# Expert gate and up weights read in 8 KB runs, and one activation table for exponential and logarithm, in a hybrid attention/GLA/MoE step

## Chip, cores and metric

The kernel runs on one core of a Trainium2 chip. A time is what the device takes for one execution, in microseconds (us); timed runs are given as their median. A profile is one further execution, recorded by the hardware profiler; its times are us from the start of its span. TensorE is PE in the profile (its weight loads PEld), VectorE is DVE, ScalarE is ACT, GpSimd is POOL, SyncE is SP; a name with a q at its end (SPq, POOLq) is that engine's instruction queue.

## The reference, cut to what matters

One layer of an encoder for 256 prompt tokens and 8 x 16 sample tokens, 384 in all, with D = 2048. All arrays are float32.

```
sh1, sc1, gt1, sh2, sc2, gt2 = split(silu(c) @ w_ada + b_ada)        # adaLN, w_ada 2048 x 12288
h = rmsnorm(x) * (1 + sc1) + sh1
z = h @ w_in                                                        # 2048 x 4368
group A: sliding-window attention with sinks
group B: lg = log_sigmoid(ab @ w_gate_up + b_gate) / 16             # decay of the gated linear attention
         b = cumsum(lg);  q*exp(b), k*exp(-b), recurrence over blocks of 16
x = x + gt1 * (concat(A, rmsnorm_head(B) * silu(r)) @ w_out)
h = rmsnorm(x) * (1 + sc2) + sh2
router: softmax over 4 groups, best group; in it the best 2 of 8 experts, softmax over the two
expert e: (silu(h @ w_eg[e]) * (h @ w_eu[e])) @ w_ed[e]             # 2048 x 512, 2048 x 512, 512 x 2048
x = x + gt2 * (sum over the two experts of gate * expert)
y = rmsnorm(x) * g_final
```

Every norm is an inverse root of a mean square. There are 32 experts; the kernel reads the weights of all of them, 12.6 MB each.

## The kernel before

Each engine has its program, written out by hand, and waits on semaphores. The order of the work is therefore the order in each engine's program.

**The ring.** All weights pass through `ring`, in units of 1 MiB (128 partitions x 8 KB, `unit(s)`). Before the experts it has 8 units (`PRE`), in the expert stage 12 (`RING`, `UE`), one expert's worth: units 0 to 3 are the gate weights, 4 to 7 the up weights, 8 to 11 the down weights. SyncE issues one DMA a unit (`fetch`, line 332, for adaLN, input and output projection; `expert`, line 392, for the experts) and waits before each on `unit_used`, which TensorE raises when it has used the unit's last bytes. A unit of expert e is thus requested when the same unit of expert e - 1 has been used. The first expert's 12 units are requested before the router has finished.

**Gate and up weights.** The view `eg_v` takes row k*128 + p of a 2048 x 512 matrix to partition p; `quad(j)` receives four neighbouring k, so each partition gets four runs of 512 floats (2 KB). The adaLN and down weights come as one run of 2048 floats (8 KB) per partition.

**The expert loop.** GpSimd gathers an expert's rows by an indirect DMA into `xg[u]` (up to 64 slots; a row's two halves of 1024 columns on partitions 0 to 63 and 64 to 127). TensorE transposes it in eight steps (`rows_T`, line 1081), ScalarE and VectorE copy the result into `xeT[u]` (lines 1339 and 1797), whose index is chunk c, half q, slot s. `up` (line 1097) multiplies: for unit j and its part kk_, `k = 4 * (j % 4) + kk_`, the rows are chunk `k % 8` of half `k // 8`. ScalarE takes the exponential (line 1343), VectorE makes silu times up (lines 1802 to 1805), TensorE transposes the hidden rows (line 1105), and `down` (line 1117) multiplies them by the down weights. Results are copied (lines 1810 and 1354) and scattered by GpSimd. TensorE's order is: up of e, transposes of e + 1, hidden transpose of e, down of e. The loops over a data-dependent overflow count follow; in the profiled run they aren't entered.

**ScalarE and its tables.** ScalarE computes exponentials and logarithms by a table that has to be loaded first. No load is written in the program: they are put in when it is built. An inverse root is `inv_rms` (lines 1154 and 1157): exp(-0.5 * ln(mean)), refined by five small steps on VectorE (`refine`, lines 1414 to 1418). It is used at the first norm, three times for the heads (`head_norms`), ahead of the experts, and three times at the end, once for each block of 128 tokens. Log-sigmoid (`log1p_exp`, lines 1253 to 1255) is |x|, exp, ln, once for each block; `decay_exps` (lines 1269, 1270) follows.

**The end.** VectorE combines the experts' outputs of each block (lines 1857 to 1859) and then refines the norm of the block before; for blocks 0 and 1 ScalarE multiplies by the norm (line 1399) and GpSimd by the gain (line 650), for block 2 VectorE does both (line 1852). GpSimd issues the output DMAs (line 652).

Of the kernel before, what the change touches and what calls it, by code (L numbers as in the profile page):

```python
# [103 lines left out]
def encoder_step(nc, A, O):  # L104
    with ExitStack() as ctx:
# [50 lines left out]
        def unit(s):  # L156
            return ring[:, s * D:(s + 1) * D]
# [124 lines left out]
        out_v = w_out.rearrange("(k p) c -> p k c", p=P)  # L282
        eg_v = A["w_expert_gate"][0].rearrange("e (k p) f -> p e k f", p=P)
        eu_v = A["w_expert_up"][0].rearrange("e (k p) f -> p e k f", p=P)
        ed_v = A["w_expert_down"][0].rearrange("e (k p) d -> p e k d", p=P)
# [34 lines left out]
        def _(sp):  # L320
# [49 lines left out]
            def expert(e, first):  # L370

                for j in range(UE):
# [12 lines left out]
                    if j < 8:  # L385
                        src = (eg_v if j < 4 else eu_v)[:, bass.ds(e, 1), 4 * (j % 4):4 * (j % 4) + 4, :]
                        src = src.rearrange("p e k f -> p (e k) f")
                        dst = quad(j)
                    else:
                        src = ed_v[:, bass.ds(e, 1), j - 8, :].rearrange("p e d -> p (e d)")  # L390
                        dst = unit(j)
# [8 lines left out]
            with sp.If(n_over > 0):  # L400
                with sp.Fori(0, n_over) as i:
                    e = sp.value_load(ov_i[0:1, bass.ds(i + 1, 1)], min_val=0, max_val=NE - 1)
                    for j in range(UE):
                        sp.wait_ge(unit_used, U_MOE + UE * (NE - 1) + UE * i + j + 1)
                        if j < 8:
                            src = (eg_v if j < 4 else eu_v)[:, bass.ds(e, 1), 4 * (j % 4):4 * (j % 4) + 4, :]
                            src = src.rearrange("p e k f -> p (e k) f")
                            dst = quad(j)
                        else:
                            src = ed_v[:, bass.ds(e, 1), j - 8, :].rearrange("p e d -> p (e d)")  # L410
                            dst = unit(j)
                        sp.dma_start(dst, src).then_inc(loaded[j], 16)
# [246 lines left out]
        def _(pe):  # L659
# [418 lines left out]
            def rows_T(u, e, gat_need):  # L1078
                pe.wait_ge(gat[u], gat_need)
                for c in range(8):  # L1080
                    last = tr(bank[c // 4][:, (c % 4) * P:(c % 4 + 1) * P], xg[u][:, c * P:(c + 1) * P], ident[:, :])  # L1081
                last.then_inc(eT_ps, 1)
# [63 lines left out]
        def _(act):  # L1146
# [4 lines left out]
            def inv_rms(sq, n_done, cols, out, n):  # L1151
# [5 lines left out]
                af(rs[:, 0, out], rs[:, 0, out], ACT.Exp, scale=-0.5).then_inc(rstd, 1)  # L1157

            rcount = [0]
            act.wait_ge(cT_ps, 1)  # L1160
# [732 lines left out]
```

## Time and profile before

| | |
|---|---|
| median of 3 timed runs | 2103.36 us (2103.22 to 2106.18) |
| the profiled execution | 2098.72 us, of which the span is 2097.1 us |
| mean granted TensorE clock | 0.913 of full speed |
| TensorE busy | 1637.1 us (78%) |
| VectorE, ScalarE, GpSimd busy | 379.5, 233.1, 175.6 us |
| moved by DMA | 602.96 MB in 213,869 packets, 288 GB/s over the span |
| TensorE matmuls of line 1097 (gate and up) | 485.1 us |
| TensorE matmuls of line 1117 (down) | 270.0 us |
| gate, up, down weights: request to landing | 19.0, 15.4, 15.3 us (128 units each) |

The span falls into a stage in which the adaLN weights stream in (to about 112 us), the input projection and attention (to about 610), the gated linear attention (to about 710), the output projection (729 to 896), norm and router (to 1001), the experts (1001 to 2033) and the end. The page cuts the span in 40 equal slices of 52.4 us, and gives for each the busy share in tenths and the transfer rate. The DMA share is the mean over 16 DMA engines; it can pass 1 where transfers overlap. The chain of waits is followed back from the last instruction, and credits each stretch to whoever released the next; it does not say what would have been late next.

### The profile page before, as it was taken

How to read it: one execution, taken by the hardware profiler on the slowest of the kernel's cores; microseconds unless marked ns; L12 is line 12 of the kernel's file. 1: busy time of each engine (PE TensorE's matmuls, PEld its weight loads, DVE VectorE, ACT ScalarE, POOL GpSimd, SP SyncE). 2: the span in 40 equal slices, each digit the busy share in tenths (PEclk: the TensorE clock that was granted, in tenths of full speed). 3: DMA queues.
4: the chain of work that ended last, by engine and by line, in shares of the span. 5: the costliest groups of instructions: out<-in, count | busy, mean ns of one | idle time of the engine just before them, and what ended most of it. 6: DMA issues, size and time to landing. Idle time of an engine off the chain costs nothing.

```text
span 2097.1 us, 22209 instructions
## 1 busy us (share of the span) xinstructions
PE 1637.1 (78%) x8832; PEld 820.6 (39%) x8832; DVE 379.5 (18%) x815; ACT 233.1 (11%) x532; POOL 175.6 (8%) x350
## 2 busy tenths in 40 slices
PE   4689999999977499985887787777877777777750
PEld 0155554444445244444443343333333333343320
DVE  1010000051824300044101101011010110101105
ACT  2110000000543100021000000000000000000004
POOL 5020000000020100002011010010100101011002
PEclk9799999999988699955899999999999999999985
DMA  9975666223970521161899999999999999999973
GB/s 330 404 259 226 258 247 247 97 99 110 412 267 13 180 94 67 40 240 41 316 399 396 398 393 397 397 396 399 393 397 395 396 398 390 398 396 396 397 278 143
DMA packets 213869, 602.96 MB, mean 288 GB/s; under 512 B 18485, under 2 KB 20597, under 8 KB 182713
## 3 DMA queue, kind: packets, MB, share of 16 engines
q1 hardware_dynamic: 197362, 559.13, 70.4%
q0 software_dynamic: 15648, 36.94, 5.1%
q10 hardware_dynamic: 816, 6.29, 0.7%
q8 instruction: 29, 0.48, 0.1%
q14 instruction: 14, 0.11, 0.0%
HBM read 595.42 MB, written 28.10 MB: 297 GB/s over the span
## 4 chain that ended last, share of the span: by engine, by line
PE 48%; DMA 37%; DVE 8%; ACT 3%; issue 2%; SPq 1%; POOL 1%; POOLq 0%; DVEq 0%; ACTq 0%
DMA ring<-in_w_expert_up 22%; PE bank L1117 9%; PE bank L1016 8%; PE bank L736 8%; PE bank L748 8%; DMA ring<-in_w_expert_gate 7%; PE bank L1097 6%; DMA ring<-in_w_ada 5%; DVE hbuf L1803 2%; PE bank L686 2%; DMA ring<-in_w_in 1%; PE bank L717 1%; DMA xbuf<-in_x_sample 1%; SPq L392 1%; PE bank L1105 1%
## 5 line engine op out<-in xcount | busy, mean ns | idle before, releaser
L1097 PE MATMUL bank<-ring,zbuf 128*64 128x256 f32 x4096 | 485.1, 385 | 137.6 <-DMA ring<-in_w_expert_up 113.1
L1097 PEld LDWEIGHTS bank<-ring,zbuf 128*64 128x64 f32 x4096 | 283.6, 138 | 346.9 <-DMA ring<-in_w_expert_up 165.5
L1117 PE MATMUL bank<-ring,hbuf 128*64 128x512 f32 x1024 | 270.0, 688 | 17.0 <-ACT hbuf L1351 17.0
L736 PE MATMUL bank<-hbuf,ring 128*128 128x384 f32 x512 | 166.1, 487 | 7.3 <-DMA ring<-in_w_in 4.4
L1016 PE MATMUL bank<-ring,hbuf 128*128 128x512 f32 x384 | 166.9, 598 | 5.7 <-DVEq L1678 5.7
L748 PE MATMUL bank<-ring,hbuf 128*128 128x512 f32 x384 | 165.8, 593 | 4.8 <-ACT xbuf L1202 3.5
L1117 PEld LDWEIGHTS bank<-ring,hbuf 128*64 128x64 f32 x1024 | 82.8, 157 | 184.7 <-issue 183.3
L686 PE MATMUL bank<-ring,dbuf 128*32 128x512 f32 x768 | 110.0, 681 | 49.2 <-DMA ring<-in_w_ada 49.2
L736 PEld LDWEIGHTS bank<-hbuf,ring 128*128 128x128 f32 x512 | 96.9, 190 | 77.5 <-issue 8.0
L1802 DVE TENSOR_SCALAR hbuf<-hbuf 128x256 f32<-128x256 f32 x32 | 9.4, 294 | 607.2 <-ACT hbuf L1343 607.2
L1016 PEld LDWEIGHTS bank<-ring,hbuf 128*128 128x128 f32 x384 | 73.6, 192 | 99.8 <-issue 92.5
L748 PEld LDWEIGHTS bank<-ring,hbuf 128*128 128x128 f32 x384 | 72.6, 190 | 98.1 <-issue 92.1
L607 POOL CAST cur<-stab 128x1 int32 (+1 forms) x32 | 5.8, 180 | 927.3 <-DVE zbuf L1810 927.3
L1343 ACT ACTIVATE hbuf<-bank 128x256 f32<-128x256 f32 x32 | 12.3, 385 | 597.4 <-PE bank L1097 597.4
L1105 PE MATMUL bank<-ident,hbuf 128*128 128x128 f32 x64 | 15.7, 331 | 79.5 <-DVE hbuf L1805 79.5
L1810 DVE COPY zbuf<-bank 128x512 f32<-128x512 f32 x32 | 22.1, 691 | 288.1 <-PE bank L1117 288.1
L686 PEld LDWEIGHTS bank<-ring,dbuf 128*32 128x32 f32 x768 | 19.5, 115 | 105.9 <-DMA ring<-in_w_ada 70.9
L1803 DVE RECIPROCAL hbuf<-hbuf 128x256 f32<-128x256 f32 x32 | 56.1, 1753 | 1.1
L1081 PE MATMUL bank<-ident,zbuf 128*128 128x128 f32 x264 | 36.9, 284 | 19.3 <-DMA zbuf<-h_rows,cur 19.3
L1354 ACT COPY zbuf<-bank 128x512 f32<-128x512 f32 x32 | 18.8, 586 | 276.5 <-PE bank L1117 276.5
L1081 PEld LDWEIGHTS bank<-ident,zbuf 128*128 128x128 f32 x264 | 29.0, 143 | 33.2 <-issue 33.2
L1105 PEld LDWEIGHTS bank<-ident,hbuf 128*128 128x128 f32 x64 | 7.0, 152 | 87.1 <-DVE hbuf L1805 87.1
(368 smaller groups left out, 1109.8 us busy)
## 6 DMA issues: line engine op xcount, KB each, us to landing
ring<-in_w_expert_gate SPq DMA_DIRECT2D x128, 1024.0 KB, 19.0
ring<-in_w_expert_up SPq DMA_DIRECT2D x128, 1024.0 KB, 15.4
ring<-in_w_expert_down SPq DMA_DIRECT2D x128, 1024.0 KB, 15.3
ring<-in_w_ada SPq DMA_DIRECT2D x96, 1024.0 KB, 11.8
ring<-in_w_in SPq DMA_DIRECT2D x34, 1024.0 KB, 10.5
ring<-in_w_out SPq DMA_DIRECT2D x16, 1024.0 KB, 5.1
ring<-y_rows ACTq DMA_DIRECT2D x3, 2048.0 KB, 12.1
h_rows<-zbuf POOLq DMA_DIRECT2D x3, 1024.0 KB, 5.6
```

Source lines behind the costliest of these rows:

```text
L392: sp.dma_start(dst, src).then_inc(loaded[j], 16)
L686: last = mm(bank[b][32 * q:32 * q + 32, :], cT[:, k, :], unit(n % PRE)[:, q * QN:(q + 1) * QN], start=(k == 0), stop=(k == KC - 1))
L717: last = mm(bank[t][:, 0:256], hT[:, k, t * P:(t + 1) * P], w[:, kk_, :], start=(k == 0), stop=(k == KC - 1))
L736: last = mm(bank[c][:, 0:TOK], w[:, kk_, c * P:(c + 1) * P], hT[:, k, :], start=(k == 0), stop=(k == KC - 1))
L748: last = mm(bank[t][:, :], hT[:, k, t * P:(t + 1) * P], w[:, kk_, :], start=(k == 0), stop=(k == KC - 1))
L1016: last = mm(bank[3 * b + t][:, :], hT[:, k, t * P:(t + 1) * P], w[:, kk_, :], start=(k == 0), stop=(k == KC - 1))
L1081: last = tr(bank[c // 4][:, (c % 4) * P:(c % 4 + 1) * P], xg[u][:, c * P:(c + 1) * P], ident[:, :])
L1097: last = mm(bank[2 + u][64 * q:64 * q + 64, 256 * (j // 4):256 * (j // 4) + 256], xeT[u][:, k % 8, k // 8, :], w[:, kk_, 256 * q:256 * q + ...
L1105: last = tr(bank[4][:, c * P:(c + 1) * P], hid[u][:, c * P:(c + 1) * P], ident[:, :])
L1117: last = mm(bank[5 + n][64 * q:64 * q + 64, :], hidT[u][:, k % 2, k // 2, :], unit(8 + k)[:, 1024 * q + QN * n:1024 * q + QN * n + QN], st ...
L1803: link(v.reciprocal(sg[u], sg[u]))
L1810: cp(ysb[u][:, 0:QN], bank[5][:, :]).then_inc(y_v, 1)
```

## The change

Two edits that don't touch each other.

1. Gate and up weights: the row of a matrix is now split as (g, p, r, c) with g and r of 2, p of 128 and c of 4, so that partition p gets rows 1024 g + 8 p + 4 r + c. Unit j holds g = j % 4 // 2 and r = j % 2: the four values of c are four neighbouring rows, one run of 2048 floats (8 KB), of every 16 KB. So that the columns of x meet the same rows, `rows_T` transposes columns at a step of 8: chunk c of the transposed rows is columns c, c + 8, c + 16, ... of the half. `up` is unchanged.
2. ScalarE asks once, before its first exponential, for the table set that has both exponential and logarithm.

```diff
-        eg_v = A["w_expert_gate"][0].rearrange("e (k p) f -> p e k f", p=P)
-        eu_v = A["w_expert_up"][0].rearrange("e (k p) f -> p e k f", p=P)
+        eg_v = A["w_expert_gate"][0].rearrange("e (g p r c) f -> p e g r (c f)", g=2, r=2, c=4)
+        eu_v = A["w_expert_up"][0].rearrange("e (g p r c) f -> p e g r (c f)", g=2, r=2, c=4)
...
                     if j < 8:
-                        src = (eg_v if j < 4 else eu_v)[:, bass.ds(e, 1), 4 * (j % 4):4 * (j % 4) + 4, :]
-                        src = src.rearrange("p e k f -> p (e k) f")
-                        dst = quad(j)
+                        src = (eg_v if j < 4 else eu_v)[:, bass.ds(e, 1), j % 4 // 2, j % 2, :].rearrange("p e f -> p (e f)")
+                        dst = unit(j)
...
             def rows_T(u, e, gat_need):
                 pe.wait_ge(gat[u], gat_need)
+                rows = xg[u].rearrange("p (n c) -> p c n", c=8)
                 for c in range(8):
-                    last = tr(bank[c // 4][:, (c % 4) * P:(c % 4 + 1) * P], xg[u][:, c * P:(c + 1) * P], ident[:, :])
+                    last = tr(bank[c // 4][:, (c % 4) * P:(c % 4 + 1) * P], rows[:, c, :], ident[:, :])
                 last.then_inc(eT_ps, 1)
...
+            nc.scalar.preload_act_table_set("natural_log_exp_and_others")
             rcount = [0]
             act.wait_ge(cT_ps, 1)
```

The load of the overflow loop is changed in the same way.

## Rows read from the trace of the kernel before

**Rows 1.** The page, 40 slices: DMA busy tenths and GB/s.

```profile
DMA  9975666223970521161899999999999999999973
GB/s 330 404 259 226 258 247 247 97 99 110 412 267 13 180 94 67 40 240 41 316 399 396 398 393 397 397 396 399 393 397 395 396 398 390 398 396 396 397 278 143
```

**Rows 2.** Who waited for whom: us in total, times, longest us.

```profile
PE bank L1097 <- DMA ring<-in_w_expert_up: 113.1, 113, 2.3
```

**Rows 3.** Chain of waits: start us, us, what (longest pieces, whole span).

```profile
1028.95 13.84 PE bank L1097 x128
1055.83 13.84 PE bank L1097 x128
...
1147.45 16.57 DMA ring<-in_w_expert_up
...
1409.89 16.58 DMA ring<-in_w_expert_up
```

**Rows 4.** Windows: us, busy us (count) by engine, PEclk, DMA share, GB/s.

```profile
72.97:92.88 19.91, 13.76 (x80) 3.68 (x80) 0.69 (x1) 2.35 (x4) 0.00 (x0) 0.83 1.01 421
1147.40:1409.80 262.40, 200.33 (x1362) 99.39 (x1360) 33.43 (x48) 15.44 (x32) 22.30 (x49) 0.95 1.04 396
...
1030.00:1060.00 30.00, 27.05 (x204) 14.77 (x202) 4.18 (x6) 1.93 (x4) 5.42 (x11) 0.94 1.04 396
```

**Rows 5.** Windows of 2 us inside one expert, the same columns.

```profile
1396.00:1398.00 2.00, 0.75 (x7) 0.51 (x5) 1.78 (x2) 0.74 (x2) 0.00 (x0) 1.00 1.00 411
...
1404.00:1406.00 2.00, 2.00 (x12) 0.74 (x10) 0.00 (x0) 0.00 (x0) 0.00 (x0) 1.00 1.04 384
...
1416.00:1418.00 2.00, 1.13 (x12) 0.46 (x8) 0.00 (x0) 0.00 (x0) 0.00 (x0) 1.00 1.03 356
...
1426.00:1428.00 2.00, 1.48 (x14) 1.05 (x16) 0.00 (x0) 0.00 (x0) 0.00 (x0) 1.00 1.03 430
```

**Rows 6.** Chain of waits just before the experts.

```profile
998.22 1.96 PE bank L1081 x8
```

**Rows 7.** ScalarE, groups by line: count, busy us, mean ns, idle us before.

```profile
L1154 ACT ACT_TABLE_LOAD x8 | 10.3, 1283 | 0.1
L1157 ACT ACT_TABLE_LOAD x8 | 10.3, 1283 | 0.1
...
L1255 ACT ACT_TABLE_LOAD x3 | 3.8, 1283 | 0.1
...
L1254 ACT ACT_TABLE_LOAD x2 | 2.6, 1283 | 0.0
...
L1161 ACT ACT_TABLE_LOAD x1 | 1.3, 1283 | 1.0 <-PEq L1882 1.0
L1269 ACT ACT_TABLE_LOAD x1 | 1.3, 1283 | 0.0
```

**Rows 8.** Timeline, gated linear attention: start us, us, instruction, [idle before it <-releaser].

```profile
626.01 3.78 PE L876 MATMUL bank<-modr,ring 128*128 128x512 f32 x4 [7.97 <-ACT ring L1270]
```

**Rows 9.** Timeline, first refining step at head norms and at the expert norm.

```profile
655.50 0.16 DVE L1414 TENSOR_SCALAR rs<-stat 128x4 f32<-128x4 f32 x1
...
668.78 0.17 DVE L1414 TENSOR_SCALAR rs<-stat 128x4 f32<-128x4 f32 x1 [1.56 <-ACT rs L1157]
...
689.23 0.17 DVE L1414 TENSOR_SCALAR rs<-stat 128x4 f32<-128x4 f32 x1 [0.58 <-ACT rs L1157]
...
905.85 0.17 DVE L1414 TENSOR_SCALAR rs<-stat 128x3 f32<-128x3 f32 x1 [2.96 <-ACT rs L1157]
```

**Rows 10.** Timeline, the end of the kernel.

```profile
2064.93 4.68 POOL L650 TENSOR_TENSOR xbuf<-xbuf,hbuf 128x2048 f32<-128x2048 f32 x1 [29.74 <-ACT xbuf L1399]
2065.29 6.47 DVE L1858 TENSOR_TENSOR ring<-ring,dbuf 128x2048 f32<-128x2048 f32 x1
...
2077.10 4.50 POOL L650 TENSOR_TENSOR xbuf<-xbuf,hbuf 128x2048 f32<-128x2048 f32 x1 [6.54 <-ACT xbuf L1399]
...
2082.06 0.15 DVE L1414 TENSOR_SCALAR rs<-stat 128x1 f32<-128x1 f32 x1 [7.14 <-ACT rs L1157]
```

More of the change, by code:

```diff
@@ L405, in _ @@
                         if j < 8:
-                            src = (eg_v if j < 4 else eu_v)[:, bass.ds(e, 1), 4 * (j % 4):4 * (j % 4) + 4, :]
-                            src = src.rearrange("p e k f -> p (e k) f")
-                            dst = quad(j)
+                            src = (eg_v if j < 4 else eu_v)[:, bass.ds(e, 1), j % 4 // 2, j % 2, :].rearrange("p e f -> p (e f)")
+                            dst = unit(j)
                         else:
```

## The prediction

> **What bounds the kernel now.** I read the page's slices first, since they show at a glance which resource is full where [rows 1]. From slice 21 to slice 38 the DMA digit is 9 and the rate stays at 390 to 399 GB/s: nearly half of the span is one stage, the 32 experts, and it runs at the pace of the transfers. The waits say the same from the other side: TensorE, at the gate and up matmuls of line 1097, waits mostly for up weights that have not landed [rows 2]. So the first part of the change (how gate and up weights are read) bears on the bound of the longest stage, and the second part (table loads on ScalarE) does not bear on that stage at all, because the expert loop uses only the exponential and copies.
>
> The chain of waits gives the lengths that I need. The piece that begins with the landing of an up weight repeats every expert; from 1147.45 to 1409.89 [rows 3] lie eight experts (the window over them counts 1362 TensorE instructions [rows 4], and an expert has 128 + 32 + 8 + 2 = 170), so one takes 262.4 / 8 = 32.8 us. The same chain holds a stretch in which TensorE did not have to wait, because the ring of 12 units had been filled ahead: expert 1 starts its gate matmuls at 1028.95 and expert 2 at 1055.83, so TensorE with its hidden-layer wait needs 26.9 us an expert. The transfers need 32.8, TensorE 26.9: the cover is 5.9 us an expert.
>
> **Part 1: the pieces.** A gate or up unit is 1 MiB (1.049 MB). Before, it is four runs of 2 KB for each partition, after, one run of 8 KB. The destination, the matmuls, the number of DMAs (12 an expert) and the bytes are the same. What does a unit cost in either form? For 8 KB runs the trace has the adaLN weights: from 72.97 to 92.88 the stage takes hardly anything else, and the window over these eight units shows 421 GB/s [rows 4], that is 19.91 / 8 = 2.49 us a unit. For the mix of the expert stage, the window over the eight experts shows 396 GB/s at a DMA share of 1.04. 32.8 us at 396 GB/s are 12.99 MB, of which the 12 units are 12.58; the 0.41 MB left are the gathered and scattered rows, 1.0 us. If the four down units (8 KB runs already) cost what the adaLN units do, 4 x 2.49 = 10.0 us, then the eight gate and up units cost 32.8 - 10.0 - 1.0 = 21.8 us, or 2.73 us each, 384 GB/s. Two-microsecond windows inside one expert bear this out: 384 GB/s where gate and up units are moving, and 411 and 430 at the times when down units are [rows 5].
>
> After the change all 12 units are of the 8 KB form: 12 x 2.49 + 1.0 = 30.9 us an expert, 1.92 less before rounding. 31 experts are loaded while the stage runs (the first lies in the ring before it starts): 31 x 1.92 = **60 us**. Is the new period still that of the transfers? TensorE needs 26.9, so 4.0 us of cover are left of 5.9. That number was taken at a granted clock of 0.94 (the window that begins at 1030 [rows 4]), no better than the 0.95 of the stage, so it is not flattered by the clock. Does the queue run dry when it moves faster? At the moment the last up unit lands, TensorE has consumed everything before it, so nearly the whole ring, twelve units or 30 us of work, is outstanding; the pause for the hidden layer (about 6 us) is far shorter. So the faster transfer is worth its full amount until TensorE binds.
>
> The bounds. The reading is now 8 KB from every 16 KB of DRAM, whereas one before unit was a run without a gap; no row shows that stride. The nearest are the adaLN units (8 KB from every 48 KB, 421 GB/s) and the down units (8 KB without a gap, mixed with others, 411 at the low one of their windows). At 411 a unit costs 2.55 us, the period is 31.6 and the gain 31 x 1.2 = 37 us. At the other end, all the bytes of the stage, about 31 x 12.99 = 403 MB, at 421 GB/s take 957 us, where they take 1017 at 396; that is again 60, and if the small transfers suffer less too (the window at 430), some 8 more. I take 60, since the adaLN row is the only one with a single form in it; 37 and 68 are kept for the range.
>
> The change also turns the rows of `xg` for the eight transposes of an expert: each now reads 128 columns at a step of 8 elements instead of neighbouring ones. No row has a strided weight load here. The transposes take 1.96 us for the first expert, at a reduced clock [rows 6]; doubled they would add 2 us there, once, since the first expert has nothing to hide them behind. Later they lie between the up matmuls and the hidden layer, where TensorE idles for VectorE anyway, and behind that is the 4.0 us of cover. Between 0 and 2, I take 0: the count of elements read doesn't change.
>
> **Part 2: the table loads.** The groups by line list all the loads: 8 + 8 + 3 + 2 + 1 + 1 = 23, each 1283 ns [rows 7]. One stays (the set asked for once, ahead of the first exponential, while ScalarE waits for the transposed conditioning vectors). 22 x 1.283 = 28.2 us of ScalarE go, but what counts is who waits. The loads stand back to back with their neighbours, so each is worth 1.283 us at most.
>
> - Log-sigmoid, lines 1254, 1255 and 1269: six loads in a row. TensorE at line 876 waits 7.97 us for what follows them [rows 8]. 6 x 1.283 = 7.7 fits inside that wait: 7.7 us.
> - Head norms, lines 1154 and 1157, three pairs of 2.57 us. What waits is VectorE's line 1414 [rows 9]. At 655.50 it shows no wait at all: 0. At 668.78 it waited 1.56, the rest was its own earlier work: 1.56. At 689.23 it waited 0.58: 0.58. A chain of waits would credit both pairs in full; next late is VectorE's queue, so I take the idle time.
> - Norm before the experts, at 905.85: VectorE idle 2.96, so the whole pair, 2.57.
> - First norm: the adaLN transfers, at a DMA digit of 9 in slice 1 [rows 1], set the end of that stage: 0. If their cover were gone it would be 2.57.
> - Final norms: for tokens 0 and 1 VectorE is busy anyway: 0. For the third, VectorE waited 7.14 us for ScalarE [rows 10], so 2.57 seem free. But at 2065.29 a VectorE operation of two SBUF operands that meets GpSimd's multiply took 6.47 us and ended 2.15 after GpSimd, where its kind takes 2.3: it stood still for as long as GpSimd ran. GpSimd's next multiply ends at 2077.10 + 4.50 = 2081.60. VectorE's five small steps would now start at 2079.5 and stop there; only about 0.8 us come through.
>
> Sum: 7.7 + 1.56 + 0.58 + 2.57 + 0.8 = **13.2 us**, between 11 and 15. The Trainium skill (ScalarE: Activation LUTs, What ACT_TABLE_LOAD costs) puts a switch at about 2.66 us, the load and a drain of 1.38. By that the path would win about twice as much, 27 us, an estimate from that page; the trace has 1283 ns and no gap beside it, so it does not enter the sum.
>
> Together 60 + 13.2 = 73.2 us. The profiled execution took 2098.7 (span 2097.1, and 1.6 around it), so it would be 2025.5. It lies 4.7 below the median of the three timed ones, 2103.4; with the same distance the median is 2103.4 - 73.2 = **2030**.
>
> **The rivals.**
> *Only the tables* (7%). The 384 GB/s of gate and up could come from something other than the length of the runs: SBUF port traffic from TensorE, which reads all along, or the mixing with row gathers. Against it: the down units flow in the same loop at 411 to 430. Then 2103.4 - 13 = 2090. The Trainium skill (DMA: Bandwidth & Descriptors, Specifications) gives 512 B as the least transfer for full line rate, by which 2 KB would already be enough and this would be the outcome; rows 5 speak against it.
> *Only the pieces* (10%). If the table set is still switched at each norm (the single request does not keep later switches from being placed), part 2 gives nothing: 2103.4 - 60 = 2043.
> *Half* (9%). TensorE becomes the bound in part of the stage because its clock falls as it idles less; the new period would be near 31.8: gain 31 x 1.0 + 13 = 44, or less, down to 30 with both: 2060 to 2073.
> *Slower* (6%). [...] The price from the slowest window of an expert, 356 GB/s [rows 5]: 2.95 us a unit, 0.22 more for each of 31 x 8 = 248 units, +55, less 13: 2145. It decides from 13.2 / 248 = 0.053 us a unit on, at 2.78 us or 377 GB/s. [...] Against it: adaLN at a pitch of 48 KB.
>
> **How the numbers follow.** The forecast, 2018 to 2045, has 66%; 2% are left for things not thought of. The range must take in only-the-pieces and the nearer half of *half*, and the bound of 37 us (2053): 2018 to 2062. What this measurement can tell from no change is about 0.2%, 4 us. All cases but *slower* and the unforeseen are faster by more: 0.92; same 0.02; slower 0.06.
>
> **What would show it.** In the profile after: one table load on ScalarE; 8 KB packets nearly everywhere and 256 x 384 = 98,000 fewer packets (four runs of each partition become one); a window over eight experts at 415 to 421 GB/s and a period of 30.9 us; TensorE at line 1097 still released by up weights; VectorE's line 1414 at the second and third head norm no longer waiting for ScalarE. A period of 32.8 with 8 KB packets would refute part 1, a release of line 1117 or 1097 by nothing but TensorE itself would say that it has become the bound, and a VectorE tail that gains all of 2.57 us would refute the port argument.

## The result and the profile after

| | before | after |
|---|---|---|
| timed runs, median | 2104.8 us (4 runs, 2103.2 to 2107.7) | 2036.7 us (4 runs, 2033.9 to 2038.1) |
| ratio | | 0.9673, 95% interval 0.9657 to 0.9690 |
| profiled execution | 2098.7 us | 2036.3 us |
| ScalarE busy | 233.1 us | 204.7 us |

The forecast was 2030, between 2018 and 2062. The gain is 68.1 us where 73.2 had been worked out, and it has the two parts that were named, with sizes of their own.

The page of the changed kernel first: span, granted clock, DMA share and rate in 40 slices (of 50.9 us now), and packets.

```profile
span 2034.6 us, 22249 instructions
...
PEclk9789999999998689975699999999999899999985
DMA  9984666522793243061599999999999999999963
GB/s 319 398 295 150 256 255 255 179 96 92 296 364 95 90 169 103 0 238 72 189 420 420 421 421 421 421 421 421 421 420 420 417 418 421 419 417 419 418 245 141
DMA packets 115566, 602.96 MB, mean 296 GB/s; under 512 B 18486, under 2 KB 20598, under 8 KB 51642
```

Against [rows 1] the expert stage (slices 21 to 38) has gone from 390 to 399 up to 417 to 421 GB/s, with the same bytes in 98,303 fewer packets. It is still bound by transfers. Two windows with the columns of [rows 4], one over the eight adaLN units, one over eight experts:

```profile
72.97:92.88 19.91, 12.19 (x80) 3.32 (x80) 0.69 (x1) 2.37 (x5) 0.00 (x0) 0.91 1.02 423
1148.92:1397.92 249.00, 198.00 (x1362) 100.53 (x1360) 33.48 (x49) 15.41 (x32) 22.34 (x48) 0.95 1.01 421
```

Both have 421 or more: gate and up weights now move like the adaLN weights, which was the assumption under the forecast. The chain of waits (start, length, what) has the same repeating piece as in [rows 3], now 27 to 29 us long instead of 15 to 17:

```profile
1148.92 28.17 DMA ring<-in_w_expert_up
1179.12 29.09 DMA ring<-in_w_expert_up
1211.18 28.18 DMA ring<-in_w_expert_up
...
1397.92 28.18 DMA ring<-in_w_expert_up
```

From 1148.92 to 1397.92 eight experts pass: 31.13 us each, where 32.8 had been measured and 30.9 forecast.

The length of the whole expert stage can be read from one row of each kernel: the gate and up matmuls, with min, median and longest duration in ns, and the start of the first and the last of them. Before, and after:

```profile
L1097 PE MATMUL bank<-ring,zbuf x4096: 379/379/688, 1001.0 to 2019.2; 128*64 128x256 f32 x196
```

```profile
L1096 PE MATMUL bank<-ring,zbuf x4096: 379/379/688, 991.4 to 1957.1; 128*64 128x256 f32 x196
```

That is 1018.2 and 965.7 us. By such first and last starts the two profiled executions come apart as follows (the stretches cover the whole span):

| stretch | before | after | difference | forecast |
|---|---|---|---|---|
| start to first long projection (line 736) | 143.6 | 147.3 | +3.7 | 0 |
| to log-sigmoid (first Abs on ScalarE) | 468.3 | 469.7 | +1.4 | 0 |
| to the output projection | 117.3 | 106.3 | -11.0 | -9.8 |
| to the first gate matmul | 271.8 | 268.1 | -3.7 | -2.6 |
| first to last gate or up matmul | 1018.2 | 965.7 | -52.5 | -60 |
| to the end of the span | 77.9 | 77.5 | -0.4 | -0.8 |
| span | 2097.1 | 2034.6 | -62.5 | -73.2 |

So the tables gave somewhat more than forecast, the runs of 8 KB gave less, and a third piece of +5 lies in the first two stretches, where the forecast had both edits at nothing. The two parts alone add up to 67.6 us, and the medians differ by 68.1. The experiments take these in turn.

### The profile page after: what moved, and what is told of

Same layout as the page of the kernel before. It is cut to its first block, busy times and chain, and to the rows that moved or that the text cites. A ratio compares the mean times of both kernels' runs of the same rounds, so it can differ in the third digit from the quotient of the medians.

```text
span 2034.6 us, 22249 instructions
## 1 busy us (share of the span) xinstructions
PE 1634.4 (80%) x8832; PEld 829.0 (41%) x8832; DVE 381.3 (19%) x815; ACT 204.7 (10%) x510; POOL 175.4 (9%) x350
## 4 chain that ended last, share of the span: by engine, by line
DMA 47%; PE 42%; DVE 5%; issue 2%; ACT 1%; SPq 1%; POOL 1%; POOLq 0%; DVEq 0%; ACTq 0%
DMA ring<-in_w_expert_up 39%; PE bank L734 8%; PE bank L1014 8%; PE bank L746 8%; PE bank L1096 6%; DMA ring<-in_w_ada 5%; PE bank L684 2%; PE bank L1116 2%; DMA ring<-in_w_in 1%; PE bank L715 1%; DMA xbuf<-in_x_sample 1%; PE bank L1031 1%; SPq L391 1%; DVE ring L1858 1%; PE bank L1032 1%
## 5 line engine op out<-in xcount | busy, mean ns | idle before, releaser
L1096 PE MATMUL bank<-ring,zbuf 128*64 128x256 f32 x4096 | 476.5, 384 | 92.5 <-DMA ring<-in_w_expert_up 85.1
L734 PEld LDWEIGHTS bank<-hbuf,ring 128*128 128x128 f32 x512 | 97.7, 192 | 77.9 <-issue 9.5
L1080 PE MATMUL bank<-ident,zbuf 128*128 128x128 f32 x264 | 39.0, 292 | 17.9 <-DMA zbuf<-h_rows,cur 17.8
L1080 PEld LDWEIGHTS bank<-ident,zbuf 128*128 128x128 f32 x264 | 32.6, 195 | 31.8 <-issue 30.9
## 6 DMA issues: line engine op xcount, KB each, us to landing
ring<-in_w_ada SPq DMA_DIRECT2D x96, 1024.0 KB, 10.3
ring<-in_w_in SPq DMA_DIRECT2D x34, 1024.0 KB, 10.7
```

Of the source, the lines that this page charges most:

```text
L734: last = mm(bank[c][:, 0:TOK], w[:, kk_, c * P:(c + 1) * P], hT[:, k, :], start=(k == 0), stop=(k == KC - 1))
L1080: last = tr(bank[c // 4][:, (c % 4) * P:(c % 4 + 1) * P], rows[:, c, :], ident[:, :])
L1096: last = mm(bank[2 + u][64 * q:64 * q + 64, 256 * (j // 4):256 * (j // 4) + 256], xeT[u][:, k % 8, k // 8, :], w[:, kk_, 256 * q:256 * q + ...
```

## Experiments

Stage lengths below are those of the table: the row of gate and up matmuls for the experts, first and last starts of others for the rest. They come from one profiled execution each. Where a median with a ratio is given, the kernel was timed in rounds beside the kernel before; the others have one time. The expert stage repeats closely: in the seven profiles of kernels with runs of 8 KB and one scatter it is 965.2 to 966.0 us, in the three with runs of 2 KB 1018.0 to 1018.2. The stretch from log-sigmoid to the output projection does not: in the eleven kernels without table loads at the second and third head norm it lies between 105.3 and 107.8 us, and the changed kernel itself has 106.3 and 107.8.

### The changed kernel again, and each part alone

No edit in the first.

> The changed kernel as it is, for a measure of the run-to-run spread of its parts. Theory A (the first 350 us, which neither edit touches, vary by themselves): the output of the stage before the first long projection group starts anywhere from 143 to 150 us. Theory B (the single table request or the changed loads disturb the start): it lies again near 147.3, where the kernel before has 143.6. Both: about 68 us below the kernel before, an expert period of 31.1 us.

Measured: 2038.7 us median, ratio 0.9709 (0.9673 to 0.9744); expert stage 965.4 us; the first long projection starts at 145.5, between the two values at issue. In the fourteen profiles shown here that start lies between 143.6 (the kernel before) and 149.1; the kernel of part 1 alone, without the table request, has 145.9, that of part 2 alone, with the old weight loads, 146.1. Part 1 cannot act there (in the changed kernel the first expert weights are requested at 870 us), so the 145.9 shows that this start varies by 2.3 us at least without any cause in the change. Theory A, that the kernel before happened to be profiled in an execution with an early start, is the likelier one. It is not settled: the kernel before has one profile, and its start is the earliest of the fourteen.

```diff
-            nc.scalar.preload_act_table_set("natural_log_exp_and_others")
```

> Part 1 alone: 8 KB runs, tables switched as before (23 loads). By my theory 53 us below the kernel before: the expert period is 31.1 us as in the changed kernel (12 units at 2.49 us and 1.26 us for the gathered and scattered rows), against 32.8. Rival (the tables help the expert stage too): the period stays above 31.1.

Measured: 2055.2 us median, ratio 0.9762 (0.9730 to 0.9795), 49 us below the kernel before. The row of its gate and up matmuls:

```profile
L1096 PE MATMUL bank<-ring,zbuf x4096: 379/379/687, 1010.1 to 1975.5; 128*64 128x256 f32 x196
```

965.4 us, the same as with both parts: the tables do nothing for the experts, and the rival falls.

```diff
+            nc.scalar.preload_act_table_set("natural_log_exp_and_others")
```

(in the kernel before, nothing else changed)

> Part 2 alone: 2 KB runs, one table load. By the reading of who waits, 13 us below the kernel before (7.7 at log-sigmoid, 1.6 + 0.6 at the head norms, 2.6 at the expert norm, 0.8 at the end), expert period 32.8. Rival (every load counts, 22 x 1.283): 28 us. Rival (the chain of waits as it is credited: all but the first norm, the first head norm and the final norms of blocks 0 and 1): 18 us.

Measured: 2091.1 us median, ratio 0.9943 (0.9921 to 0.9966), 13.0 us below. Its row:

```profile
L1097 PE MATMUL bank<-ring,zbuf x4096: 379/379/689, 992.3 to 2010.3; 128*64 128x256 f32 x196
```

1018.0 us. By the interval the gain is 7 to 17 us: the count of all loads (28 us) and the chain's credit (18) are both outside; 13 was the forecast for this part.

### How the rate depends on the length of a run

Four kernels, in which a unit of gate or up weights takes, for each partition, four runs of 2 KB, two of 4 KB, one of 8 KB (the changed kernel) or, in a DMA of two units, one of 16 KB. All read the same 16 KB regions and transpose x at a step of 8. The 2 KB kernel, in short:

```diff
-        eg_v = A["w_expert_gate"][0].rearrange("e (g p r c) f -> p e g r (c f)", g=2, r=2, c=4)
+        eg_v = A["w_expert_gate"][0].rearrange("e (g p s r) f -> p e g r s f", g=2, s=4, r=2)
...
-                                      xeT[u][:, k % 8, k // 8, :], w[:, kk_, 256 * q:256 * q + 256],
+                                      xeT[u][:, 2 * kk_ + j % 2, k // 8, :], w[:, kk_, 256 * q:256 * q + 256],
```

> As the changed kernel, with the same rows of x and the same 16 KB regions, but a unit takes four runs of 2 KB at a step of 4 KB for each partition instead of one of 8 KB. If the length of the runs sets the rate, the expert period is 32.8 us, as before the change. If it was the order in which memory is read, or the layout of the transposes, it is near 31.1.

```profile
L1096 PE MATMUL bank<-ring,zbuf x4096: 379/379/687, 997.1 to 2015.2; 128*64 128x256 f32 x196
```

1018.1 us: the length of the kernel before to 0.1, though the order of reading and the transposes are those of the changed one. The length of the run is the cause, and nothing else of the first edit.

```diff
-        eg_v = A["w_expert_gate"][0].rearrange("e (g p r c) f -> p e g r (c f)", g=2, r=2, c=4)
+        eg_v = A["w_expert_gate"][0].rearrange("e (g p s r c) f -> p e g r s (c f)", g=2, s=2, r=2, c=2)
...
-                                      xeT[u][:, k % 8, k // 8, :], w[:, kk_, 256 * q:256 * q + 256],
+                                      xeT[u][:, 4 * (kk_ // 2) + 2 * (j % 2) + kk_ % 2, k // 8, :], w[:, kk_, 256 * q:256 * q + 256],
```

> The same with two runs of 4 KB at a step of 8 KB. If the cost is a fixed time for each run (0.20 us a unit more for four times the runs), a unit costs 2.49 + 0.07 us and the period is 31.7. If there is a threshold below 4 KB: 31.1.

```profile
L1096 PE MATMUL bank<-ring,zbuf x4096: 379/379/687, 993.4 to 1976.6; 128*64 128x256 f32 x196
```

983.2 us, a period of 31.7: the value for a fixed cost of each run, not that of a threshold. The steps are 34.9 us from 2 to 4 KB and 17.8 from 4 to 8 (965.4, the changed kernel's second run). The 31 experts that load during the stage save 63,488 runs in the first and 31,744 in the second, so the price is about the same for each: spread over 16 DMA engines, 8.8 and 9.0 ns a run.

```diff
-        eg_v = A["w_expert_gate"][0].rearrange("e (g p r c) f -> p e g r (c f)", g=2, r=2, c=4)
+        eg_v = A["w_expert_gate"][0].rearrange("e (g p rc) f -> p e g (rc f)", g=2, rc=8)
...
-                for j in range(UE):
+                for j in [*range(0, 8, 2), *range(8, UE)]:
...
-                        sp.wait_ge(unit_used, U_MOE + UE * (e - 1) + j + 1)
+                        sp.wait_ge(unit_used, U_MOE + UE * (e - 1) + j + 1 + w2)
...
-                        dst = unit(j)
+                        dst = ring[:, j * D:(j + 2) * D]
```

(`w2` is 1 for gate and up units, 0 for down units; TensorE waits for the double unit's semaphore)

> Gate and up weights in DMAs of 2 MiB, with one run of 16 KB for each partition. The expert stage took 1018.1 us with runs of 2 KB, 983.2 with 4 KB and 965.4 with 8 KB, which fits a fixed cost for each run: halving the number of runs once more would take 8.8 us off, 956.6. If a transfer is cut into packets of 8 KB anyway, 965.4. A DMA of two units is issued one unit later than before; if that lets the queue run low, it is above 965.4.

```profile
L1098 PE MATMUL bank<-ring,zbuf x4096: 379/379/688, 992.4 to 1952.6; 128*64 128x256 f32 x196
```

960.2 us, 5.2 less than at 8 KB. The packets fell from 115,565 to 97,133, so a run of 16 KB does travel as one; but the next 15,872 runs saved in the stage brought 5.2 ns each and not 9.0. None of the three expectations is met. A part of what is missing is the later request of a double unit: in the first 100 us of the stage this kernel moves 389 GB/s at a DMA share of 0.93, the changed one 393 at 0.96, which is about 1 of the missing 3.7 us. Between that and the last 30 us it moves 423 against 420. The rest stays open.

The packet records of the traces show the price of a run directly. Between 1148 and 1397 us a packet of 2 KB takes 88.6 ns on the mean (kernel before), one of 4 KB 163.2 (the 4 KB kernel), one of 8 KB 313.5 (the changed one) and one of 16 KB 614.5 (this one). Two packets of one size thus take 14.0, 12.9 and 12.5 ns more than one of the next: for the engine that carries it the price does not fall at 16 KB. The stage shows less than that throughout (8.8, 9.0 and 5.2); by the DMA share, above 1 in all four windows (1.04, 1.02, 1.01, 1.01), packets of an engine overlap a little.

```diff
-        eg_v = A["w_expert_gate"][0].rearrange("e (g p r c) f -> p e g r (c f)", g=2, r=2, c=4)
+        eg_v = A["w_expert_gate"][0].rearrange("e (g r p c) f -> p e g r (c f)", g=2, r=2, c=4)
...
-                rows = xg[u].rearrange("p (n c) -> p c n", c=8)
+                rows = xg[u].rearrange("p (r n c) -> p r c n", r=2, c=4)
```

> Runs of 8 KB that follow each other, so that a unit is 1 MiB without a gap, instead of 8 KB of every 16 KB (transposes then at a step of 4). If the gap costs nothing the period is 31.1 and the time that of the changed kernel within 0.2%. If the gap costs, it is below 31.1, and each 0.1 us of it is 3 us.

Measured: 2038.7 us median, ratio 0.9674 (0.9650 to 0.9699), as the changed kernel (0.9673).

```profile
L1096 PE MATMUL bank<-ring,zbuf x4096: 379/379/687, 1004.1 to 1969.9; 128*64 128x256 f32 x196
```

965.8 us. The 8 KB hole behind each run costs nothing: the rival that would have ended slower has no ground here.

### What the row transfers of an expert cost

```diff
             def scatter(idx, u):
                 settle(1)
-                g.indirect_dma_start(y_dram, bass.IndirectOffsetOnAxis(idx.bitcast(U32), 0), ysb[u], None,
-                                     bounds_check=pairs_max, oob_is_err=False).then_inc(sct[u], 16)
+                for out in (y2_dram, y_dram):
+                    g.indirect_dma_start(out, bass.IndirectOffsetOnAxis(idx.bitcast(U32), 0), ysb[u], None,
+                                         bounds_check=pairs_max, oob_is_err=False).then_inc(sct[u], 16)
```

(and the waits on `sct` doubled)

> The changed kernel with every scatter of an expert's results done twice, the second time to an array that nobody reads. If a gather or a scatter holds the weights up by 0.63 us, as the intervals between units show, the period is 31.1 + 0.6 = 31.7 us. If they go beside the weights for the 0.2 MB they carry, it is 31.1 + 0.5; if they are hidden, 31.1.

```profile
L1098 PE MATMUL bank<-ring,zbuf x4096: 379/379/687, 990.2 to 1976.1; 128*64 128x256 f32 x196
```

985.9 us, 20.5 more than the 965.4 of the changed kernel's second run, for 31 or 32 scatters: 0.64 to 0.66 us each, the value read from the intervals. The price of a gather is not tested by it; both are read in the timeline below.

### Table loads put back

```diff
                 act.wait_ge(sq, n_done)
+                if rcount[0] in (0, 1, 5, 6):
+                    nc.scalar.preload_act_table_set("exp_and_others")
+                    nc.scalar.preload_act_table_set("natural_log_exp_and_others")
```

> The changed kernel with two table loads put back ahead of each of four norms: the first one, the first head norm, the final norms of blocks 0 and 1 (8 loads, 10.3 us of ScalarE). By the reading that VectorE or the transfers are what is late there, each costs nothing: from log-sigmoid to the first output-projection matmul 106 to 107 us, the part after the last down matmul 64.4 us, as in the changed kernel. By the reading that a load delays what follows it, 2.6 us more in the first of these and up to 5.1 in the second.

Measured, one execution: log-sigmoid to output projection 105.3 us, the part after the last down matmul 64.5 us; the first long projection starts at 146.3. Eight loads, 10.3 us of ScalarE, cost nothing that shows: VectorE's first refining step at the first head norm (at 659.69) still has no wait before it. The 105.3 by itself would prove little, since this execution was spared the fall of the clock that the next run is about, worth 2.4 us. The whole took 2043.0 us, 6.7 more than the changed kernel's profiled execution; the attention stretch, which holds no load, is 10.7 longer in it (110.6 against 99.9 us) and is taken up below. Its tail shows the same stop of VectorE as the changed kernel's (next section).

```diff
+                if rcount[0] in (2, 3):
+                    nc.scalar.preload_act_table_set("exp_and_others")
+                    nc.scalar.preload_act_table_set("natural_log_exp_and_others")
```

> The changed kernel with two loads put back ahead of the second and of the third head norm. By the waits of VectorE in the kernel before, the two pairs bring 1.56 and 0.58 us of wait back: log-sigmoid to the first output-projection matmul 2.1 us longer than in the changed kernel (106.3). By the credit of the chain of waits 5.1 us longer.

The timeline of this kernel, VectorE's first refining step and TensorE's matmuls between the two norms:

```profile
662.77 0.17 DVE L1417 TENSOR_SCALAR rs<-stat 128x4 f32<-128x4 f32 x1 [1.57 <-ACT rs L1159]
...
672.65 1.96 PE L913 MATMUL bank<-xbuf,ring 128*128 128x256 f32 x8 [0.77 <-ACT hbuf L1298]
...
674.55 1.93 PE L934 MATMUL bank<-dbuf,ring 128*32 128x256 f32 x32
...
683.23 0.17 DVE L1417 TENSOR_SCALAR rs<-stat 128x4 f32<-128x4 f32 x1 [0.58 <-ACT rs L1159]
```

The waits came back to the hundredth: 1.57 and 0.58. But the stretch from log-sigmoid to the output projection took 106.2 us, as without them. Both expectations are missed, though 2.1 us is no more than this stretch varies by; what settles it are the rows. The same rows of the changed kernel, with the expert norm's below them:

```profile
661.34 0.17 DVE L1414 TENSOR_SCALAR rs<-stat 128x4 f32<-128x4 f32 x1
...
671.23 3.75 PE L913 MATMUL bank<-xbuf,ring 128*128 128x256 f32 x8 [0.77 <-ACT hbuf L1295]
...
674.91 2.54 PE L934 MATMUL bank<-dbuf,ring 128*32 128x256 f32 x32
...
683.52 0.16 DVE L1414 TENSOR_SCALAR rs<-stat 128x4 f32<-128x4 f32 x1
...
897.74 0.17 DVE L1414 TENSOR_SCALAR rs<-stat 128x3 f32<-128x3 f32 x1 [0.60 <-ACT rs L1156]
```

and TensorE's of the kernel before:

```profile
678.67 1.97 PE L915 MATMUL bank<-xbuf,ring 128*128 128x256 f32 x8 [0.77 <-ACT hbuf L1295]
...
680.56 1.93 PE L936 MATMUL bank<-dbuf,ring 128*32 128x256 f32 x32
```

Without the loads VectorE waits nowhere and the work reaches TensorE 1.4 us earlier; the eight matmuls of line 913 then take 3.75 us instead of 1.96 and the next 32 take 2.54 instead of 1.93. That is a granted clock of 1.2 GHz in place of 2.4 for some 5 us (the mean from 670 to 678 is 0.61 and 0.84 of full speed), and 2.4 us lost. Counted from log-sigmoid, the second norm's row comes 1.7 us earlier without the loads (44.39 against 46.09 us) and the third norm's at the same time (66.57 and 66.55). Of the eleven kernels without loads at these two norms ten have 3.75 us there; the eleventh, with loads put back where they are free, has 1.97, and its stretch from log-sigmoid to the output projection is the shortest, 105.3 us. The three with loads (before, the runs of 8 KB alone, this one) have 1.96 and 1.97. What TensorE did before is much the same in both: it had been idle for 3.6 us with the loads gone and for 5.3 with them (its wait for line 1579), then worked through eight small matmuls and eight transposes. So the clock falls in nearly all of the one kind and in none of the other, and where it falls it takes back the 2.1 us that had been won. That the removed waits cause the fall is argued from this pattern and not shown; the one exception shows that they do not force it.

### The end of the kernel

```diff
                 refine(t + 6, slice(t, t + 1), slice(t, t + 1), D)
-                if t < 2:
-
-                    dve.nop().then_inc(fin_rs, 1)
-                    return
                 stt(x[:, t, :], x[:, t, :], rs[:, 0, t:t + 1], gfin, ALU.mult, ALU.mult).then_inc(fin_rdy, 1)
```

(and ScalarE's multiplication by the norm and GpSimd's by the gain taken out)

> The changed kernel, with the final norm and gain of blocks 0 and 1 done as for block 2, in one VectorE operation of 2.35 us, instead of ScalarE (2.0) and GpSimd (4.5). If VectorE stands still while GpSimd multiplies, line 1858 of block 2 takes 2.3 us instead of 6.47, and the last output DMA is issued about 5 to 6 us earlier after the first gated block: 0.25 to 0.3% faster than the changed kernel. If the 6.47 us have another reason, VectorE has 2 x 2.35 us more and the end comes no earlier.

Measured: 2033.0 us median, ratio 0.9671 (0.9649 to 0.9692); the changed kernel beside it had 2038.7. The part after the last down matmul is 58.3 us instead of 64.4. VectorE in its timeline:

```profile
2006.84 2.29 DVE L1848 TENSOR_TENSOR ring<-ring,dbuf 128x2048 f32<-128x2048 f32 x1
...
2015.55 2.35 DVE L1842 SCALAR_TENSOR_TENSOR xbuf<-xbuf,rs,hbuf 128x2048 f32<-128x2048 f32 x1
```

Line 1848 is the old 1858: 2.29 us, not 6.47, with GpSimd silent. The port argument holds. This version is 5.7 us faster than the changed kernel by the medians and 6.1 by the profile; the intervals of the two ratios overlap (0.9649 to 0.9692, 0.9709 with 0.9673 to 0.9744), so it is the profile that shows it.

### All of it together

Runs of 16 KB for gate and up as above, the down weights in the same form, and the tail on VectorE:

```diff
-        ed_v = A["w_expert_down"][0].rearrange("e (k p) d -> p e k d", p=P)
+        ed_v = A["w_expert_down"][0].rearrange("e (q p c) d -> p e q (c d)", q=2, c=2)
...
+                cols = hid[u].rearrange("p (n c) -> p c n", c=2)
                 for c in range(2):
-                    last = tr(bank[4][:, c * P:(c + 1) * P], hid[u][:, c * P:(c + 1) * P], ident[:, :])
+                    last = tr(bank[4][:, c * P:(c + 1) * P], cols[:, c, :], ident[:, :])
```

> The changed kernel with three things more: gate and up weights in DMAs of 2 MiB with runs of 16 KB, the down weights too (two neighbouring rows for each partition, hidden rows transposed at a step of 2), and the final norm and gain of all blocks on VectorE. Runs of 16 KB for gate and up took the expert stage from 965.4 to 960.2 us; a third of the units more should give half of that again, 957.6. The part after the last down matmul 58.3 us instead of 64.4. Together 14 us below the changed kernel, about 0.963 of the kernel before. If the down weights in pairs come too late for the down matmuls, the stage is above 960.2.

Measured: 2021.7 us median, ratio 0.9623 (0.9600 to 0.9647).

```profile
L1095 PE MATMUL bank<-ring,zbuf x4096: 379/379/687, 992.9 to 1948.1; 128*64 128x256 f32 x196
```

The expert stage is 955.2 us, 5.0 below the kernel with 16 KB for gate and up alone and better than the 957.6 expected; the part after the last down matmul 58.1. It beats the kernel before by 3.8% and the changed one by 15 us by the medians (taken beside different runs of the kernel before: 0.9623 against 0.9673, with intervals that do not meet).

## Why the prediction came out as it did, point by point

**The bound of the expert stage.** Right. The stage kept waiting for up weights, [rows 2] has its counterpart in 85.1 us of waits after (113.1 before), and TensorE did not become the bound except at the start, where the ring has a lead: the first four experts of the changed kernel take 27 to 28 us each, as the first three did before.

One step of the argument does not fit the kernel before: that nearly the whole ring, 30 us of work, is outstanding when TensorE waits. An up unit landed 15.4 us after its request there. The rest of the ring was requested late: SyncE's queue spent nearly the whole period in the instructions that issue the DMAs:

```profile
1403.02 12.16 SPq L392 DMA_DIRECT2D ring<-in_w_expert_up  x4
1415.35 4.36 SPq L392 DMA_DIRECT2D ring<-in_w_expert_down  x4
1420.26 15.56 SPq L392 DMA_DIRECT2D ring<-in_w_expert_gate  x4
```

That opens a rival for the whole of part 1, which no run tests alone: that issuing DMAs of many runs set the pace, and not carrying them. The trace of before speaks against it. The shortest issue of a gate unit took 0.37 us, so that issuing by itself does not need the 2.3 us of the median, let alone the 3 to 4 in these rows; units landed 15 us after their request, so that the transfers had work in hand; and the DMA share of 1.04 has the engines busy throughout. In the changed kernel gate and down units land 26 us after their request, and the step is then true.

**Gate and up at the adaLN rate.** Right, and shown: 2 KB runs give 1018.1, 8 KB runs 965.4 with the rest of the kernel the same. The unit itself now costs what the forecast said. TensorE's gate and up matmuls in the changed kernel, each group of 16 started by the landing of a unit (in brackets the wait and its releaser):

```profile
1443.54 1.95 PE L1096 MATMUL bank<-ring,zbuf 128*64 128x256 f32 x16 [0.41 <-DMA ring<-in_w_expert_gate]
1446.01 1.95 PE L1096 MATMUL bank<-ring,zbuf 128*64 128x256 f32 x16 [0.53 <-DMA ring<-in_w_expert_gate]
1449.11 1.95 PE L1096 MATMUL bank<-ring,zbuf 128*64 128x256 f32 x16 [1.16 <-DMA ring<-in_w_expert_up]
1452.25 1.95 PE L1096 MATMUL bank<-ring,zbuf 128*64 128x256 f32 x16 [1.19 <-DMA ring<-in_w_expert_up]
1454.76 1.95 PE L1096 MATMUL bank<-ring,zbuf 128*64 128x256 f32 x16 [0.56 <-DMA ring<-in_w_expert_up]
```

The starts are 2.47, 3.10, 3.14 and 2.51 us apart: 2.49 for a unit, as from [rows 4], and 0.63 more in two of the intervals.

**The term that was mis-sized** is what the row transfers of an expert add: 1.0 us, worked out as the 0.41 MB left over at 396 GB/s. The forecast had not looked at single units. Before the change:

```profile
1411.87 1.95 PE L1097 MATMUL bank<-ring,zbuf 128*64 128x256 f32 x16 [0.76 <-DMA ring<-in_w_expert_gate]
1415.19 1.95 PE L1097 MATMUL bank<-ring,zbuf 128*64 128x256 f32 x16 [1.37 <-DMA ring<-in_w_expert_gate]
1418.51 1.95 PE L1097 MATMUL bank<-ring,zbuf 128*64 128x256 f32 x16 [1.37 <-DMA ring<-in_w_expert_up]
1421.16 1.95 PE L1097 MATMUL bank<-ring,zbuf 128*64 128x256 f32 x16 [0.71 <-DMA ring<-in_w_expert_up]
```

The intervals are 3.32, 3.32 and 2.65. In the changed kernel the packets of one scatter and one gather (issued at 1441.46 and 1443.11) move between 1445 and 1451, inside the two long intervals. So a gather or a scatter cost 0.66 us each and not 0.5, 1.3 together, and a gate or up unit only 2.66 to 2.69 and not 2.73. With 12 x 2.49 + 1.26 = 31.14 the new period would have come out as measured (31.13), and the gain as 31 x 1.66 = 51 us; the stage gave 52.5. The doubled scatter confirms the price: 0.65 us for a transfer that carries 0.197 MB (6.30 MB more in all, over 32 experts) and at the rate of the weights would take 0.47. The remainder that was split by bytes should have been split by time.

**The steps and bounds at nothing.** The gap of 8 KB costs nothing (965.8 without it). The strided transposes cost nothing that the stage shows: with 2 KB runs and strided transposes it is 1018.1, without them 1018.2. The weight load of such a transpose did become longer, 193 ns by the median instead of 141, but the eight of the first expert take 1.95 us, as before (1.94). The bound of 411 GB/s was too low for runs of 8 KB: in its window of [rows 5], 1396 to 1398, the packet records have 73 packets of 2 KB beside 82 of 8 KB, while the window at 1426 (430 GB/s) has 105 of 8 KB alone. The Trainium skill (DMA: Bandwidth & Descriptors, Specifications) has 512 B as the least transfer for full rate; here runs of 2 KB, four times that, are still slower than runs of 8 KB, by 5% of the stage, and the measurement decides. The Trainium skill (DMA: Bandwidth & Descriptors, Why small descriptors are slow (HBM only)) names a fixed overhead for each packet, about three cycles; the trace agrees that there is a fixed cost for each, 12.5 to 14.0 ns by the packet records and 8.8 or 9.0 ns a run by the stage.

**Table loads.** The sum of 13.2 was right in size: 13.0 by the medians of the kernel with that part alone. Its terms were not all right. Log-sigmoid: ScalarE's first Abs and TensorE's matmuls that wait for line 1270, after the change:

```profile
616.95 0.60 ACT L1253 ACTIVATE ring<-bank 128x512 f32<-128x512 f32 x1 [2.34 <-PE bank L859]
...
623.19 1.98 PE L874 MATMUL bank<-modr,ring 128*128 128x512 f32 x4 [1.42 <-ACT ring L1270]
```

6.24 us apart, where 14.07 had lain between 611.94 and the row of [rows 8]: 7.8 for 7.7, or 1.3 us for each of the six loads. The prediction's estimate of twice as much in all (27 us) is not borne out. Up to the first head norm 3.0 us more came off, which the forecast did not have: the four matmuls take 1.98 us instead of 3.78 [rows 8], and the ones behind them are shorter too. The granted clock in the 5 us from 623 is 1.00 in the changed kernel, after an idle time of 1.4 us; in the 5 us from 626 before it was 0.55, after one of 8.0 us. The second execution of the changed kernel has 1.8 instead of 3.0; its clock is at 0.52 between 630 and 636. At the head norms the reading of the waits was right and the credit wrong: 1.56 went, as [rows 9] has it, and the clock took 2.4 back between the second and the third norm. So it is in part luck that the sum was right: what one change of the clock gave and what another took, neither in the forecast, nearly cancel. At the expert norm VectorE's wait fell from 2.96 to 0.60 and the stretch around it is 268.0 to 270.2 us in the twelve kernels without these loads and 271.8 and 272.1 in the two with them: 1.6 to 4.1, forecast 2.6. The four pairs of loads put at nothing were at nothing, shown by putting them back.

**The end.** This part of the argument came out to the tenth of a microsecond. In the changed kernel:

```profile
2003.63 6.47 DVE L1858 TENSOR_TENSOR ring<-ring,dbuf 128x2048 f32<-128x2048 f32 x1
...
2015.45 4.50 POOL L648 TENSOR_TENSOR xbuf<-xbuf,hbuf 128x2048 f32<-128x2048 f32 x1 [6.54 <-ACT xbuf L1399]
...
2017.85 0.15 DVE L1414 TENSOR_SCALAR rs<-stat 128x1 f32<-128x1 f32 x1 [4.58 <-ACT rs L1156]
2018.04 1.93 DVE L1415 TENSOR_TENSOR rs<-rs 128x1 f32<-128x1 f32 x1
```

GpSimd multiplies from 2015.45 to 2019.95. VectorE starts its refining at 2017.85; line 1414, with one operand from memory, takes 0.15 us; line 1415, with two, takes 1.93 instead of 0.16 and ends at 2019.97. Of 2.57 us saved on ScalarE, 0.8 arrive (64.4 against 65.2 after the last down matmul), as forecast. The Trainium skill (SBUF — State Buffer, SBUF: two separate sides) states that VectorE with two SBUF inputs and GpSimd share a pair of ports by an exclusive lock for the whole instruction; the trace agrees, down to the one-operand step that passes. The kernel with the loads put back ahead of the other norms has the same pair of rows:

```profile
2024.65 0.15 DVE L1417 TENSOR_SCALAR rs<-stat 128x1 f32<-128x1 f32 x1 [4.58 <-ACT rs L1159]
2024.84 1.93 DVE L1418 TENSOR_TENSOR rs<-rs 128x1 f32<-128x1 f32 x1
```

**The rivals.** Only the tables: refuted by the ladder. Only the pieces: refuted, one load is left of 23. Half: TensorE kept a clock of 0.95 in the stage and did not bind after the first four experts. Slower: the time refutes it, and the gapless kernel shows that reading 8 KB of every 16 KB costs nothing.

**The offset.** The profile of before was 6 us below its median, that of after at it. The forecast carried the distance over, and so aimed at 2025.5 for an execution whose first 617 us were then 5 us longer. The largest part of such differences sits in one place. The window from 515 to 610 us, most of the attention, in the changed kernel and in the one with loads put back where they are free:

```profile
515.00:610.00 95.00, 88.67 (x752) 45.09 (x751) 64.81 (x264) 42.76 (x181) 0.00 (x0) 0.98 0.88 343
```

```profile
515.00:610.00 95.00, 88.63 (x707) 43.62 (x709) 64.61 (x263) 41.94 (x178) 0.00 (x0) 0.91 0.86 332
```

The same work at a granted clock of 0.98 and of 0.91: the stretch takes 99.9 and 110.6 us. Of fourteen profiles nine have 99.4 to 100.9 and five have 103.5 to 110.6, with old and new tables, and with runs of 2, 8 and 16 KB, among the latter. The changed kernel and the gapless one, for example, have the same instructions up to there and 99.9 and 109.0 us. So it is a matter of the execution and not of the change, and can explain why the timed runs of one kernel spread by up to 0.9% (2030.9 to 2049.0 for the gapless one, whose profile is of its slowest run). Why the clock differs is open.

## What to carry to other kernels

In a stage bound by transfers, count the runs, not only the bytes: if two forms of the same load are in the trace, the difference between them is the price of the shorter one, and neighbouring rows can often be given to one partition by permuting the operand on the other side. When a remainder has to be split over things that share a queue, take their cost from the intervals between landings and not from their bytes. And of a stall that goes, credit only what the engine behind it waited; then look at which port and which clock the earlier start runs into.

## What was not expected of the hardware

- Each run has a fixed price on the DMA engine that carries it: 8.8 ns (2 to 4 KB) and 9.0 ns (4 to 8 KB) by the length of the stage, still 5.2 ns from 8 to 16 KB; by the packet records 14.0, 12.9 and 12.5 ns.
- With 2.1 us of waits off VectorE, TensorE's granted clock was at 1.2 GHz for about 5 us right behind in ten of eleven kernels, and at 2.4 GHz in the three that had the waits; the stretch came out as long either way (106.3 and 106.2 us). One of the eleven kept 2.4 GHz.
- A gather or scatter of some 0.2 MB of rows holds up the weights by 0.63 to 0.66 us, a third more than its bytes at their rate.
- The attention stretch of the same instructions takes 99.4 to 110.6 us, at a granted clock of 0.91 to 1.00, from one execution to the next.
